# Attention 2 of a three-block network: the division by the softmax sum moved from the powers into the turn

## What is computed

```python
scores = einsum("bnqkgd,bnskd->bnkgqs", qb, kb) * scale      # 128 queries x 256 keys
scores = where(mask, scores, -inf)
m = maximum(max(scores, axis=-1), sink)
p = exp(scores - m)
denom = sum(p, axis=-1) + exp(sink - m)
p = p / denom
out = einsum("bnkgqs,bnskd->bnqkgd", p, vb)
```

## Time and profile before

| what | value |
|---|---|
| median of 3 runs | 3037.93 us (3037.4 to 3038.45) |
| the profiled execution | 3039.63 us |
| its span | 3037.8 us |
| granted TensorE clock, mean | 0.991 |
| busy share: PE, DVE, ACT, POOL | 97%, 54%, 38%, 33% |
| attention 2 in the span, first scores to last values | 1769.1 to 1941 us |

### The profile page before, as it was taken

One profiled execution on the slowest core, in us unless ns is written; L12 is line 12 of the kernel. 1 busy time (PEld: TensorE's weight loads), 2 busy tenths in 40 slices (PEclk: granted clock), 3 DMA queues, 4 the chain that ended last, 5 costly groups with the idle time before them and its releaser, 6 DMA issues.

```text
span 3037.8 us, 37680 instructions
## 1 busy us (share of the span) xinstructions
PE 2940.9 (97%) x15094; PEld 2378.1 (78%) x15094; DVE 1638.4 (54%) x2686; ACT 1141.0 (38%) x1952; POOL 1004.6 (33%) x725
## 2 busy tenths in 40 slices
PE   8999989999999999999999999999999999999998
PEld 7876668888878888887888866677877778788887
DVE  6989760025545664224233567777656545534436
ACT  3125662222441111223333267546545422332344
POOL 3210002232417786234541212321111234442542
PEclk9999999999999999999999999999999999999999
DMA  4110001113323333113332211342222266543323
GB/s 134 49 42 22 15 15 49 49 56 111 125 78 88 89 90 102 41 55 116 107 124 77 65 31 56 115 124 67 60 65 72 71 175 168 180 141 109 110 78 111
DMA packets 267776, 260.56 MB, mean 86 GB/s; under 512 B 17457, under 2 KB 208049, under 8 KB 266577
## 3 DMA queue, kind: packets, MB, share of 16 engines
q1 hardware_dynamic: 232624, 198.15, 21.9%
q10 hardware_dynamic: 34976, 60.01, 6.2%
HBM read 213.41 MB, written 42.99 MB: 84 GB/s over the span
## 4 chain that ended last, share of the span: by engine, by line
PE 81%; DVE 9%; ACT 5%; DMA 2%; issue 2%; POOL 1%; ACTq 0%; SPq 0%; DVEq 0%
PE psum L581 24%; PE psum L582 24%; PE psum L583 24%; PE psum L587 3%; DVE arena L2971 1%; DMA arena<-in_w_in 1%; PE psum L794 1%; PE psum L764 1%; ACT WS L1240 1%; DVE arena L2428 1%; PE psum L971 1%; PE psum L995 1%; ACT arena L1435 1%; PE psum L1164 1%; DVE XL L2293 1%
## 5 line engine op out<-in xcount | busy, mean ns | idle before, releaser
L3253 POOL TENSOR_TENSOR WS<-arena,WS 128x1024 fp32r<-128x1024 f32 (+1 forms) x295 | 722.7, 2456 | 1644.9 <-ACT WS L1240 1644.8
L581 PE MATMUL psum<-XH,WS 128*128 128x512 f32 x2600 | 1031.3, 397 | 16.0 <-ACT arena L1418 3.4
L582 PE MATMUL psum<-XL,WS 128*128 128x512 f32 x2600 | 1015.5, 391 | 0.0
L583 PE MATMUL psum<-XH,WS 128*128 128x512 f32 x2600 | 1015.3, 391 | 0.0
L581 PEld LDWEIGHTS psum<-XH,WS 128*128 128x128 f32 x2600 | 490.2, 189 | 133.8 <-issue 12.9
L1240 ACT ACTIVATE WS<-arena 128x1024 fp32r<-128x1024 f32 (+1 forms) x295 | 308.2, 1052 | 738.2 <-PE psum L583 247.3
L583 PEld LDWEIGHTS psum<-XH,WS 128*128 128x128 f32 x2600 | 489.7, 188 | 103.6
L582 PEld LDWEIGHTS psum<-XL,WS 128*128 128x128 f32 x2600 | 490.4, 189 | 97.2
L581 PE MATMUL psum<-WS,XH 128*128 128x512 f32 x960 | 377.5, 393 | 9.5 <-POOL WS L3253 7.4
L582 PE MATMUL psum<-WS,XH 128*128 128x512 f32 x960 | 374.3, 390 | 0.0
L583 PE MATMUL psum<-WS,XL 128*128 128x512 f32 x960 | 374.3, 390 | 0.0
(11 more groups left out here) (300 smaller groups left out, 2875.6 us busy)
## 6 DMA issues: line engine op xcount, KB each, us to landing
arena<-in_w_in SPq DMA_DIRECT2D x85, 512.0 KB, 3.8
arena<-in_w_out SPq DMA_DIRECT2D x48, 512.0 KB, 3.7
arena<-in_w_in_even SPq DMA_DIRECT2D x48, 512.0 KB, 4.0
arena<-in_w_out_even SPq DMA_DIRECT2D x32, 512.0 KB, 3.7
h_spill<-arena ACTq DMA_DIRECT2D x24, 512.0 KB, 3.1
arena<-s_table SPq DMA_DIRECT2D x8, 1536.0 KB, 6.9
arena<-in_w_in_odd SPq DMA_DIRECT2D x18, 512.0 KB, 3.8
s_table<-arena SPq DMA_DIRECT2D x32, 256.0 KB, 3.0
```

The source lines that it names most:

```text
L581: e.matmul(ps, wh, xh, start=start, stop=False)
L582: e.matmul(ps, wh, xl, start=False, stop=False)
L583: return e.matmul(ps, wl, xh, start=False, stop=stop)
L3253: e.tensor_tensor(lo, x, hi.bitcast(F32), SUB).then_inc(*w.up("w_lo", u))
```

## The change

The powers are no longer divided in place. VectorE makes, for each unit, four diagonal matrices of 128x128 from the identity and the four reciprocals (`DIAG[u % 3]`, three buffers of 128x512 in a part of the on-chip memory that is free in this stage). The turn becomes an ordinary product of the undivided powers with the diagonal of their head, which transposes and divides.

```diff
         UNITS = [(n, g, hq) for n in range(8) for g in range(2) for hq in range(2)]
+        DIAG = [view(111.5 + 2 * i, 4, 128) for i in range(3)]
...
                     for p in range(2):
                         for k in range(2):
-                            t = tp(psum[:, bank, tile_of(2 * p + k)], PRU[u % 3][:, 2 * k + p, 128 * kb:128 * kb + 128])
+                            t = e.matmul(psum[:, bank, tile_of(2 * p + k)], PRU[u % 3][:, 2 * k + p, 128 * kb:128 * kb + 128],
+                                         DIAG[u % 3][:, 2 * k + p, :], start=True, stop=True)
                     t.then_inc(*w.up("t2", u, kb))
...
                 e.reciprocal(den, den).then_inc(*w.up("p2_rden", u))
                 w.own()
-                for i in range(4):
-                    e.tensor_scalar(pr[:, i, k0:256], pr[:, i, k0:256], den[:, i:i + 1], None, M).then_inc(
-                        *w.up("p2_n", u, i, also=[("p2_nrm", u)] if i == 3 else []))
+                e.tensor_tensor(DIAG[u % 3], ident.rearrange("p (u b) -> p u b", u=1).broadcast_to([128, 4, 128]),
+                                den.rearrange("p (a u) -> p a u", u=1).broadcast_to([128, 4, 128]), M).then_inc(
+                                    *w.up("p2_n", u, also=[("p2_nrm", u)]))
```

## The result

The changed kernel takes 3056.71 us (median of 4 runs, 3054.21 to 3060.46), the kernel before beside it 3037.66 (4 runs, 3036.31 to 3038.45): ratio 1.0061, 95% interval 1.0049 to 1.0073, so **19.05 us slower**. The forecast was 3058.1, the range 3053 to 3065.

A forecast was written before the change was run, and what follows sets the result against it. TensorE (PE), busy 97% of the span, was taken as the bound. 28.9 us added to it less 8.7 us of covered waits gave +20.2 us on a median of 3037.93, so 3058.1 us, range 3053 to 3065.

The forecast's parts named there:

- An ordinary fp32 product is two records, 0.112 us apart: Turn on PE: each product with the diagonal shows two records, 0.112 us per step, where a transpose shows one.
- 0.96 us more in a full turn, 0.50 in a small one: PE's turn: 2.05 us instead of 1.09 in 28 full units, 0.50 more in 4 small ones; 28.9 us added.
- The cover, 8.7 us: Attention 2: PE's waits shrink as PE arrives later and VectorE finishes earlier, taking 8.7 us off the added work.
- Start: Stage up to 1789 us: 1.3 us of PE's waits go, 1.0 of it at L1749.
- 1896 to 1914: Three turns there wait 1.1 us each for the division; all 3.3 us go.
- 1789 to 1896: Waits of two turns, a third turn and three filler products shrink: 3.5 us go.
- The retimed meeting: Turn at 1811.01 us: VectorE still meets GpSimd, by about 0.15 us; PE waits about 0.9 us instead of 1.69.
- VectorE's 0.45 us a unit: VectorE, full units: four divisions of 1.14 us become one product of 0.69 us, giving back 0.45 us each.
- The sum: Whole kernel: 28.9 us added to PE less 8.7 us of cover, +20.2 us.
- The waits stay: Rival, chance 0.12: meetings with GpSimd fall elsewhere, only 2 to 4 us of cover comes; +26 us, 3064 us.
- One record: Rival, chance 0.06: a product with a diagonal costs PE one record; about -4 us, 3034 us, or -7.5, 3030.4.
- Four for one: Rival, chance 0.02: each turn product takes four steps of a transpose's 0.108 us; +66.8 us, 3104.7 us.

The follow-up runs named there:

- run 3: The changed kernel with each product with the diagonal issued twice, the second over the first: 3109.35 us, ratio 1.0229.
- run 2: The changed kernel with the transposes put back, the diagonal still made and nothing divided: 3034.94 us, ratio 0.9986 to the kernel before.
- run 7: The kernel before with its four divisions writing bf16 and the turn a bf16 product with a bf16 identity: 3033.43 us, ratio 0.9981.
- run 1: The kernel before with its four divisions kept and the turn an ordinary fp32 product with the identity: 3060.23 us, ratio 1.0069.
- run 5: The kernel before with only the filler order changed, one and two pieces in turn from unit 17 on: 3041.34 us, ratio 1.0010.
- run 6: The changed kernel with powers, diagonal and turn products in bf16, plus one and two filler pieces in turn from unit 17: 3035.20 us, ratio 0.9984.

## Why the prediction was right

The likeliest case came in, by its own steps; each size stands here beside what it measured.

- *An ordinary fp32 product is two records, 0.112 us apart.* Right: 480 records, and 1.79 us for 16 of them in run 3. It was read from L1113 and L1156 alone, though the stage itself had it: the program issues four products at L971 for a unit, and the timeline shows eight records.
- *0.96 us more in a full turn, 0.50 in a small one.* Right: 1.98 against 1.02 us to the first value record, and 1.09 against 0.57. That gives 28 x 0.96 + 4 x 0.50 = 28.9 us as forecast; by the stretches PE's work in the stage grew by 187.2 - 159.0 = 28.2.
- *The cover, 8.7 us.* It was 12.9 - 3.3 = 9.6. Start: 1.3 forecast, and 1.3 measured (the first wait went from 2.32 to 2.14, that for L1749 from 1.27 to 0.28). 1896 to 1914: all 3.3, right. After it: all 0.6, right. **1789 to 1896: 3.5 forecast, 4.5 measured**, the one term that was mis-sized. The retimed meeting itself was right (0.15 us behind GpSimd, measured 0.16, and about 0.55 us behind GpSimd's end, measured 0.54), but PE waited 0.42 us there and not 0.9. I had let PE reach that turn too early. These are the scores one unit ahead of that turn, before and with the change:

```profile
1802.91 1.13 PE L971 MATMUL psum<-arena 64*128 64x256 f32 x8
...
1804.85 1.13 PE L972 MATMUL psum<-arena 64*128 64x256 f32 x8
```

  From these scores to the next PE took 5.28 us (to 1808.19), 0.52 of it the wait for L1749, and takes 5.65 now (to 1810.50): some 0.9 more of work, less the wait. So PE comes 0.4 us later to the turn, counted from the same scores, while GpSimd and the diagonal keep the places that I gave them. By the 0.9 us that the prediction leaves, PE would come no later than before. The meeting comes twice, which makes the 1.0 us.
- *VectorE's 0.45 us a unit.* The diagonal took 0.692 us, forecast 0.69. Its worth on the path was not separated in the forecast; runs 2 and 7 put it at 4.2 and 4.3 us, run 1 at 2.1 beside the products that the change has.
- *The sum.* +20.2 forecast, +19.05 measured, +18.5 in the stage. PE's work came out 0.7 us smaller and the cover 0.9 larger. The idle time of 13.7 us that the prediction starts from was counted to 1945 us and holds 0.8 us behind the stage, so its 5 us for the changed kernel are 4.2 in the stage, where 3.3 were measured; and the "other waits for VectorE", put at some 1.5 us, were 1.0. That the median came within 1.4 us of the forecast is luck in part, since the four runs of the change spread over 6.3 us.
- *The rivals.* "The waits stay" falls: 3.0 us of waits for the diagonal are left of 9.8. "One record" falls with the 480, and its price was fair: run 2, which has its PE, was 3.5 us faster than before where it said about 4 (its own terms, 0.2, twice 0.4, 0.35 and 2, add up to 3.35). "Four for one" falls, since 2.05 us against 1.09 is less than two. The Trainium skill's advice against this edit (Perfetto Trace Analysis, section Transposes) held for fp32; in bf16 the ordinary product was cheaper than the fp32 transpose, 0.62 against 1.09 us for eight, and a bf16 transpose was not tried.

## What to carry to other kernels

Before an operation is folded into a transpose, count the records of an ordinary product of the same operands elsewhere in the trace: the program showed eight products for eight transposes, and only the trace told that the price doubles. Then ask which engine pays: 0.45 us of VectorE a unit was bought with 0.96 us of PE, on a PE that is busy 97% of the span, and gave back about 2 us for 28. Where the rounding allows it, look at the same fold with bf16 operands: here it won on both engines, 9.3 us, of which run 7 puts some 5 on the cheaper product and 4.3 on the lighter VectorE.

## What the runs showed that was not expected

- Joining four VectorE instructions into one changes which meetings with GpSimd happen. One instruction of 0.69 us that started 0.39 us before GpSimd's finished in its usual time (1787.32), four in 1.1 us from the same place did not (1789.70 in run 1, 3.24 us).
- Spreading the filler more evenly moved PE's waits instead of removing them: 9.8 us before and in run 5, in nine and in six waits, and from 8.3 to 10.0 us with the products in bf16. That the first two are equal may be chance.
- The times of one kernel spread more than their medians' differences at times: run 6 had ten runs from 3029.45 to 3036.41 us with nothing between 3031.1 and 3034.7, and a mean granted clock of 0.990 to 0.992 in the four faster ones and 0.989 or 0.990 in the six slower. What sets that was not tested.
